# Rows of an expert's block dealt over the lanes in steps of six

## What is computed

```python
logit_g = h @ w_rg + b_rg                    # 4 groups, the best one is taken
logit_e = h @ w_re + b_re                    # 8 experts in each group, the best 2 of the group are taken
top_v, top_i = lax.top_k(logit_e, 2)
gate = softmax(top_v) * p_grp
# each expert e works on the tokens that chose it:
g, u = split(x[tokens of e] @ w_up[e])       # w_up[e]: 1024 x 1024
y = (silu(g) * u) @ w_down[e]                # w_down[e]: 512 x 1024
out[token] = sum over its two experts of gate * y
```

## Time and profile before

| | |
|---|---|
| three runs, us | 2897.01, 2898.96, 2906.28 (median 2898.96) |
| the profiled execution, us | 2905.13 |
| its span in the profile, us | 2903.3 |
| PE busy in the span | 95% |
| DVE, ACT, POOL busy | 52%, 27%, 2% |
| DMA moved | 422.63 MB |
| mean granted clock of TensorE | 0.979 of full speed |

### The profile page before, as it was taken

How to read it: one execution, slowest core, us unless ns; L and a number is a source line. 1 busy time by engine, 2 the same in 40 slices (tenths; PEclk the granted TensorE clock), 3 DMA queues, 4 the chain that set the end, 5 groups by cost and what they waited for, 6 DMA issues and landing times. The chain is left out here.

```text
span 2903.3 us, 43922 instructions
## 1 busy us (share of the span) xinstructions
PE 2764.1 (95%) x18251; PEld 1647.2 (57%) x18251; DVE 1502.9 (52%) x2089; ACT 776.4 (27%) x1444; POOL 66.4 (2%) x90
## 2 busy tenths in 40 slices
PE   8999889999999999999999998999999799999995
PEld 4444554444444434444454445656565799999994
DVE  7886776566666668783742008867665211111113
ACT  2111771111111114411100016656423111121111
POOL 0000000000000000000000000000000000000002
PEclk9999999999999999999999999999999899999998
DMA  3022942111111127763231000012201999999985
GB/s 144 29 73 41 272 162 73 44 44 44 44 44 44 44 81 260 269 237 117 62 98 42 10 11 1 1 46 84 91 7 59 352 397 395 396 401 398 394 331 185
DMA packets 79797, 422.63 MB, mean 146 GB/s; under 512 B 10688, under 2 KB 20416, under 8 KB 63680
## 3 DMA queue, kind: packets, MB, share of 16 engines
q1 hardware_dynamic: 58016, 362.29, 34.0%
q10 hardware_dynamic: 15664, 41.95, 4.0%
q0 software_dynamic: 6000, 16.78, 1.8%
HBM read 384.68 MB, written 51.38 MB: 150 GB/s over the span
## 5 line engine op out<-in xcount | busy, mean ns | idle before, releaser
L3555 PE MATMUL ex_up_ps<-big,ex_xT 128*32 128x384 f32 x3072 | 344.7, 489 | 12.6 <-issue 7.5
L3557 PE MATMUL ex_up_ps<-big,ex_xT 128*32 128x128 f32 x3072 | 349.0, 274 | 0.0
L3557 PEld LDWEIGHTS ex_up_ps<-big,ex_xT 128*32 128x32 f32 x3072 | 332.1, 110 | 0.5
L2204 PE MATMUL dn_acc<-big,V 128*128 128x512 f32 x506 | 220.8, 596 | 13.5 <-PEq L45 11.5
L1754 PE MATMUL fm_ring<-h,V 128*128 128x512 f32 x504 | 219.7, 592 | 0.0
L295 DVE TENSOR_SCALAR_CACHE_REDUCE h<-ad_s_ps 128x1280 f32<-128x1280 f32 x64 | 92.9, 1489 | 177.2 <-PE ad_s_ps L204 177.2
L3557 PE MATMUL ex_y_ps<-ex_wd,ex_hT 128*32 128x128 f32 x1536 | 174.4, 274 | 0.0
L2204 PEld LDWEIGHTS dn_acc<-big,V 128*128 128x128 f32 x506 | 96.4, 191 | 135.5 <-issue 131.6
L3555 PE MATMUL ex_y_ps<-ex_wd,ex_hT 128*32 128x384 f32 x1536 | 172.3, 489 | 0.8 <-DVE ex_hT L3699 0.8
L3557 PEld LDWEIGHTS ex_y_ps<-ex_wd,ex_hT 128*32 128x32 f32 x1536 | 168.6, 111 | 0.4
L1754 PEld LDWEIGHTS fm_ring<-h,V 128*128 128x128 f32 x504 | 95.8, 190 | 120.5 <-issue 120.5
(11 more groups left out here) (586 smaller groups left out, 4780.2 us busy)
## 6 DMA issues: line engine op xcount, KB each, us to landing
big<-in_w_eup SPq DMA_DIRECT2D x32, 4096.0 KB
ex_wd<-in_w_edown SPq DMA_DIRECT2D x32, 2048.0 KB, 22.5
V<-in_w_down SPq DMA_DIRECT2D x35, 704.0 KB, 5.3
dn_tail<-in_w_mod ACTq DMA_DIRECT2D x48, 512.0 KB, 4.7
fm_up<-in_w_up SPq DMA_DIRECT2D x22, 1028.0 KB, 4.9
y_dram<-in_cos SPq DMA_DIRECT2D x1, 21504.0 KB, 71.1
y_dram<-big ACTq DMA_DIRECT2D x32, 288.0 KB
dn_tail<-in_w_in SPq DMA_DIRECT2D x17, 512.0 KB, 4.5
```

The source lines that it names most:

```text
L2204: mm = nc.tensor.matmul(down_bank(kind, m), weights[:, k * P:(k + 1) * P], src[:, k, :], start=(k == 0), stop=(k == KH - 1))
L3555: nc.tensor.matmul(o[32 * g:32 * g + 32, 0:W], rows(g), w[:, 0:W], start=first, stop=last)
L3557: mm = nc.tensor.matmul(o[BR:P, g * P:(g + 1) * P], rows(g), w[:, W:BANK], start=first and g == 0, stop=last and g == GR - 1)
```

## The change

The row r of a block no longer stands in lane r. With `dealt[l] = 16 l - 95 floor(l / 6)`, lane l = 6 q + s holds row q + 16 s, for q from 0 to 15 and s from 0 to 5. The one-hot matrix `lanes` compares with `dealt` in place of the constant row 0, 1, 2, .... The slot follows: `slot += 5 row - 95 floor(row / 16)`, which is block times 96 plus the new lane. `floor` is the kernel's helper of two DVE operations, an addition and a subtraction of 12582912. Two new tiles of 128x96 hold `dealt` and `sixth`, which are made at the phase's start by five operations (one scaling, two in `floor`, two for `dealt`); five more stand before the cast of the slots, after `ids` has been written. Nothing else changes: the sizes of all transfers and products, their order and the waits.

```diff
@@ -3168,6 +3168,7 @@
         turned, evicted, both_ready, pre_ready, first_ready, lanes_ready, ids_ready, exp_in, exp_done, step = (
             ph.sem(s) for s in ("turned", "evicted", "both_ready", "pre_ready", "first_ready", "lanes_ready",
                                 "ids_ready", "exp_in", "exp_done", "step"))
+        dealt, sixth = ph.sb("dealt", [P, BR]), ph.sb("sixth", [P, BR])
         listed_ready, listed_kept, x_cleared = ph.sem("listed_ready"), ph.sem("listed_kept"), ph.sem("x_cleared")
         block_made, block_turned, block_kept = ph.sem("block_made"), ph.sem("block_turned"), ph.sem("block_kept")
         block_ps = acc[0:1, 0, 0:NB]
@@ -3365,6 +3366,10 @@
                 V_.tensor_tensor(ws[:], wr[:], wide(m(3), 36), ALU.mult).then_inc(ws_ready, 1)
                 V_.tensor_tensor(spread, ident, wide(m(5), P), ALU.mult).then_inc(spread_ready, 1)
                 st.done(V_.memset(r["ids"], T))
+                st.done(V_.tensor_scalar(sixth[:], cst["lane"][:, 0:BR], 1.0 / 6, -0.498, ALU.mult, ALU.add))
+                floor(sixth[:])
+                st.done(V_.tensor_scalar(dealt[:], cst["lane"][:, 0:BR], 16.0, None, ALU.mult))
+                st.done(V_.scalar_tensor_tensor(out=dealt[:], in0=sixth[:], scalar=-95.0, in1=dealt[:], op0=ALU.mult, op1=ALU.add))
                 for j in range(n - 1):
                     dve.wait_ge(done, j + 1)
                     V_.scalar_tensor_tensor(out=h[:, j, :], in0=acc[:, j % 2, :], scalar=m(2)[:, j:j + 1], in1=h[:, j, :],
@@ -3439,7 +3444,7 @@
                     st.done(V_.scalar_tensor_tensor(out=here, in0=wide(cst["token"], NB), scalar=-float(T), in1=here,
                                                     op0=ALU.add, op1=ALU.mult))
                     V_.tensor_tensor(lanes[:, a * TT:(a + 1) * TT, 0:BR], wide(lanef[:, a], BR),
-                                     cst["lane"][:, 0:BR].unsqueeze(1).broadcast_to([P, TT, BR]),
+                                     dealt[:].unsqueeze(1).broadcast_to([P, TT, BR]),
                                      ALU.is_equal).then_inc(lanes_ready, 1)
                 st.done(V_.tensor_copy(cnt[:, 0:1], incl[:, E_ - 1:E_]))
                 st.done(V_.tensor_scalar(cnt[:, 1:2], cnt[:, 0:1], 1.0, 0.5, ALU.add, ALU.mult))
@@ -3455,6 +3460,10 @@
                 V_.tensor_copy(r["block"][0:1, :], block_ps).then_inc(block_kept, 1)
                 dve.wait_ge(ids_ready, 1)
                 V_.tensor_scalar(r["ids"][0:BR, 0:NB], ids_ps[0:BR], float(T), None, ALU.add).then_inc(ids_kept, 1)
+                st.done(V_.tensor_scalar(blkf, lanef, 1.0 / 16, -0.498, ALU.mult, ALU.add))
+                floor(blkf)
+                st.done(V_.scalar_tensor_tensor(out=slotf, in0=lanef, scalar=5.0, in1=slotf, op0=ALU.mult, op1=ALU.add))
+                st.done(V_.scalar_tensor_tensor(out=slotf, in0=blkf, scalar=-95.0, in1=slotf, op0=ALU.mult, op1=ALU.add))
                 V_.tensor_copy(r["slot"], slotf)
```

## The result

| | before | after |
|---|---|---|
| median of six runs, us | 2897.72 | 2884.39 |
| lowest to highest, us | 2894.14 to 2906.28 | 2880.18 to 2891.16 |
| the profiled execution, us | 2905.13 | 2880.74 |

The ratio is 0.9948, 95% interval 0.9935 to 0.9960. Times 2897.72 that is 15.1 us less, 11.6 to 18.8. The forecast was 7.3 us, half of it; the time lies where the rival *PE's pace is reached* had put it (2882 to 2887).

A forecast was written before the change was run, and what follows sets the result against it. The DMA was taken to bound most expert blocks, PE a few. 7.0 us from 28 balanced blocks plus 0.3 from the first gather, operations hidden, gave -7.3 us: 2891.7 us from 2898.96, range 2882 to 2898.

The forecast's parts named there:

- PE's pace is reached: Rival, expert blocks: a row costs 0.37 us or more, every block takes 17.0 us, -12 to -17 us; chance 0.20.
- The DMA is the bound, PE is just behind: Expert blocks: DMA bounds most, PE a few; 28 windows total 492.53 us, 16.5 us above PE's pace of 17.0 each.
- Six lanes for each engine: Expert gathers: each of 16 DMA engines serves six neighbouring lanes, so ten fetch 6 rows, one 4, five none.
- The worth of the balance per block: Expert blocks: the fullest engine has 1.6 rows less, taken as 0.25 us per block, 7.0 us over 28 blocks.
- The price from the rate's dip: Upper price of a row: if the fall to 347 GB/s in each block is all the gather's, 0.44 us.
- The total of the work stays: Expert blocks: levelling only fills idle engine time, 0.25 us per block; the DMA engines' total work does not change.
- The first gather: Before the second up load: two rows less per engine start the experts 0.3 us earlier, 0.9 at the upper price.
- Ten operations in the shade: Route: five vector operations at the start, 1.35 us, and five before the slots' cast, 1.05 us, all hidden: 0.
- Common limit: Rival: rate dips come from memory or ports that all engines share; 0 to -3 us; chance 0.10.
- Deal without effect: Rival: lanes go to engines in another order, so the deal does not level them; 0 us, 2899; chance 0.05.
- Slower: Rival: an engine without rows now is the slowest and gets 4 per block; 17 to 49 us slower; chance 0.05.
- The signs in the profile: Expected afterwards: windows 17.3 us on average, late DMA share 1.01, no dips under 0.9, PE's up wait 11.9 to 6 us.

The follow-up runs named there:

- steps of twelve: Changed kernel with rows dealt in steps of twelve, fullest engine 5.9 rows: 17.60 us per block with half the down product; with all work 17.39, ratio 0.9987 to before.
- the relieved kernel: Kernels that leave out half of the down product, so PE needs 14.4 us per block: 17.62 us with before's row order, 17.07 with the change.
- experiment 2: Kernel before with half the down product and every index out of bounds, so no expert row is fetched: 15.58 us per block.
- in front: Kernel before's row order, row r in lane r and paddings last, with half of the down product: 17.62 us per block.
- experiments 1 and 3: 1: half the down product, before's order 17.62 us per block, dealt 17.07. 3: padding lanes fetch too, 17.85 and 17.89; dealt with all work, ratio 1.0028.
- experiment 5: Kernel before with half the down product and row r in lane 95 - r, paddings first: 17.41 us per block.

## Why the prediction was right and wrong

The measured time lies in the stated range, 2882 to 2898 us, but only because the range took in the rival at PE's pace. The forecast itself, 7.3 us and at most 11, had half of what came: the interval of the gain begins at 11.6. The mechanism was right, the size of its main term wasn't.

- **The DMA is the bound, PE is just behind.** Right. With PE relieved before's windows keep their 17.6 us.
- **Six lanes for each engine.** Right as far as the runs can tell: the deal that levels runs of six gains most, steps of twelve in the relieved kernel nothing. The Trainium skill (DMA: Bandwidth & Descriptors, Why a DMA increments its semaphore by 16 and not by 1) has a tile of 96 partitions split over 16 engines, and the runs agree with that. That the six lanes are neighbours is the runs' finding.
- **The worth of the balance per block.** This term was mis-sized. The prediction had three prices of a row, 0.152, 0.204 and 0.44 us, which gave 0.24, 0.33 and 0.70 us a block, and it went by the low end: "I take 0.25 us, since idle time is measured where the other is priced, and since the total of the work stays." Measured are 0.34 us a row (with all lanes full 0.38) and 0.55 us a block where PE does not limit, times 28 blocks 15.5 us, and 16.4 us in the changed kernel, where the term said 7.0. The price from the rate's dip was the nearest, as nearly the whole dip is the gather's, which experiment 2 showed. At 0.37 the rival sets in; the price lies just under it, and the DMA's pace of 17.07 came to within 0.1 us of PE's.
- **"The total of the work stays".** It doesn't, and this is where the other half of the gain was. A window times its DMA share is what the 16 engines were at work in a block. Over the last twenty windows it is 17.68 x 0.993 = 17.56 us in front, 17.09 x 1.010 = 17.26 dealt, 15.62 x 1.010 = 15.78 without rows, and 17.75 x 1.010 = 17.93 with 96 rows in front. About half of the 0.30 us between front and dealt is an effect of where the windows begin: the former hold 387.8 weight packets each, the latter 383.8, where a block has 384. Taken by packets, over the 28 blocks, the average weight packet fell from 652 to 645 ns with half of the down product, and from 653 to 640 ns from before to after; with 24 of them for each engine and block that is 0.17 and 0.32 us. With the packets of the rows (187 to 195 ns, and 192 to 182) the work fell by about 0.14 us a block in the one pair and 0.35 in the other. What is left of the 0.55 and 0.58 us, 0.4 and 0.2, is idle time that went; so the forecast's 0.25 was near for the idle time of the change, and the work was the term that it put at nothing. This fits a shorter gather, which leaves fewer weight packets to be slowed: 68 a block begin while the rows come, against 103 in front (68 and 87 with all work). In engine time, rows and slowed packets together, a fetched row costs about 0.42 us in front and 0.39 dealt, near the prediction's upper price. Why a weight packet takes longer while rows are fetched stays open.
- **The first gather.** Mis-sized, and its worth as well. 0.3 us were forecast (0.9 as the upper end), 1.04 us measured from the gather's issue to PE's first work. Without rows it takes 5.43 us, so a row costs (8.16 - 5.43) / 6 = 0.46 us there. But only 0.41 us of the 1.04 reach the blocks behind: PE's granted clock stood at 0.50 (1.2 GHz) when the experts began, after an idle wait of 9.39 us before and 8.35 after. It rose to full speed 6.2 us later before, and 7.5 us later after, so that the earlier start ran at half speed for longer. The stretch from PE's first work to the third up load's issue lasts 15.88 us at a mean clock of 0.81 before, 16.51 at 0.77 after; in both PE is busy but for 0.6 us.

```profile
2271.57:2287.45 15.88, 15.26 (x217) 14.22 (x221) 0.06 (x1) 7.04 (x18) 2.35 (x4) 0.81 0.99 369
2266.25:2282.76 16.51, 15.90 (x218) 14.70 (x221) 0.07 (x1) 7.05 (x18) 2.35 (x4) 0.77 0.98 373
```

- **Ten operations in the shade.** Right: 1.27 us (1.35 forecast) and 1.03 us (1.05), slack as read, ratio 0.9997 alone.
- **The rivals.** *PE's pace is reached* came true; 16.4 + 0.4 = 16.8 us by the profiles, inside the interval of the timed difference, 11.6 to 18.8. *Common limit* as the cause falls by experiments 1 and 3. *Deal without effect* falls by the gain. *Slower* did not come; the rows at the back give no sign of a slow engine there (experiment 5). The Trainium skill (DMA: Bandwidth & Descriptors, Latency and other measured facts) has engines 7 and 15 as usually slower. No run here shows it. If the engines are numbered along the lanes, engine 7 has six rows in front and at the back alike, so that only 15 was tried.
- **The signs in the profile.** The share late in the stretch rose to 1.011 as said. The short dips did not all go: they stand at 0.99 on average, with single ones at 0.82. PE's wait went to nothing, not to 6 us, and all windows but one stand at 17.0, which the prediction had named as the sign that the price was too low.

None of these deals beats steps of six, which is level already. The DMA's pace (17.07) and PE's (17.0) now nearly meet, so a further gain in this stretch would have to shorten both; no run tried it.

## What to carry to other kernels

Where an indirect gather skips padding lanes, deal the valid rows so that each run of lanes that one DMA engine serves has as many of them. Here it shortened each gather from 5.1 to 3.9 us. Don't price a row by its bytes at the average rate: a kernel in which all lanes skip, with the compute engine relieved, gives the price in one run. And when an imbalance is to go, don't take its idle share for the whole gain: here the work itself got less too, as the other transfers' packets are slowed only while the gather lasts.

## What the hardware did that I had not expected

- In a stretch where all 16 engines are full (share 1.01), each 4 KB row on the fullest engine adds 0.34 to 0.38 us to a block, more than twice the 0.152 us of its bytes. Its own packet takes only 0.19 us; the rest is that the 16 KB packets of the weights go from 611 ns to 750 to 800 ns while rows are fetched. The core's rate falls from 428 to 364 GB/s meanwhile, on average over the blocks.
- Fetching 96 rows, six on every engine, takes only 0.23 us a block more than 64 with ten engines at six. Fetching 64 rows, four on each, takes 0.55 us less.
- The pace of a block follows how long its gather lasts (3.9 to 5.9 us) more closely than how many rows the fullest engine has.
- A lane that the gather skips still leaves a packet of 4 bytes: the software queue has 6000 packets in every run, 4096 rows or 5216 or 2048.
- An engine that starts 1.04 us earlier from an idle wait need not be 1.04 us ahead afterwards: PE ran at a granted clock of 0.50 for 7.5 us in place of 6.2 and kept 0.41.
